# A mixing stage with its score and logarithm steps one cell ahead, and a convolution that starts in the pair before it

## The reference, cut to what matters

```python
h = rms_norm(x, norm_mix_g); proj = h @ w_in          # -> conv_in (2048), q, k, v (1024 each), gate logits (2048)
# branch 1: convolution
u = a * sigmoid(gt)                                    # a, gt: the halves of conv_in
y[c, t] = bias[c] + sum_{i<31} w[i, c] * u[c, t-30+i]  # 31 taps, each channel by itself
# branch 2: stick-breaking attention, 16 heads of 64, per query block
z = (q @ k.T) / 8                                      # causal: key < query
log_1m = where(causal, -softplus(z), 0)
after = reverse_cumsum(log_1m) - log_1m                # over the later keys
w = where(causal, exp(log_sigmoid(z) + after), 0)
o = w @ v
```

## Time and profile before

| | us |
|---|---|
| median of 3 runs | 4964.03 (4961.4 to 4964.75) |
| profiled execution, its own time | 4961.57 |
| its span, first to last instruction | 4959.8 |
| mean granted TensorE clock (of full speed) | 0.964 |
| the last output of the mixing stage is copied at | 1158.35 |

### The profile page before, as it was taken

The page is one execution under the profiler, slowest core; times in us unless marked ns, Lnnn a source line. Parts: engine busy times, 40 slices in busy tenths (PEclk is TensorE's granted clock), DMA queues, the critical chain, the costliest instruction groups (busy, mean ns, idle before and its releaser), DMA issues. The chain is left out here.

```text
span 4959.8 us, 62173 instructions
## 1 busy us (share of the span) xinstructions
PE 4612.5 (93%) x21768; PEld 3671.5 (74%) x21768; DVE 2884.2 (58%) x4467; ACT 1703.9 (34%) x2690; POOL 1781.3 (36%) x1078
## 2 busy tenths in 40 slices
PE   6999999986896987999999998999799999999998
PEld 5666666653676765888888887888688888888886
DVE  3777777776425217777777746776344444444445
ACT  3555555553524313333333333444112111111212
POOL 1443433341124115777777761111122222222221
PEclk9999999987998998999999999999899999999999
DMA  2111111103423131222222224555744444444441
GB/s 78 35 47 48 47 44 43 47 18 128 153 97 132 34 127 69 99 97 93 98 97 93 104 106 144 205 204 210 275 149 134 148 145 144 144 148 145 138 144 68
DMA packets 260002, 555.58 MB, mean 112 GB/s; under 512 B 17104, under 2 KB 148432, under 8 KB 246736
## 3 DMA queue, kind: packets, MB, share of 16 engines
q1 hardware_dynamic: 255184, 485.85, 29.1%
q10 hardware_dynamic: 4608, 67.11, 3.3%
HBM read 384.08 MB, written 168.82 MB: 111 GB/s over the span
## 5 line engine op out<-in xcount | busy, mean ns | idle before, releaser
L155 PE MATMUL expert_o<-expert_ahi,expert_vhi 128*128 128x512 f32 x2048 | 799.5, 390 | 25.8 <-POOL expert_vlo L2338 20.8
L156 PE MATMUL expert_o<-expert_alo,expert_vhi 128*128 128x512 f32 x2048 | 798.5, 390 | 0.0
L157 PE MATMUL expert_o<-expert_ahi,expert_vlo 128*128 128x512 f32 x2048 | 798.3, 390 | 0.0
L2402 DVE TENSOR_TENSOR expert_acc<-expert_acc,expert_o 128x512 f32<-128x512 f32 x496 | 341.0, 688 | 709.8 <-PE expert_o L157 704.7
L2338 POOL TENSOR_TENSOR expert_vlo<-expert_vraw,expert_vhi 128x1024 fp32r<-128x1024 f32 x128 | 323.3, 2526 | 1055.8 <-ACT expert_vhi L2356 1055.8
L155 PEld LDWEIGHTS expert_o<-expert_ahi,expert_vhi 128*128 128x128 f32 x2048 | 385.4, 188 | 108.1 <-issue 27.2
L156 PEld LDWEIGHTS expert_o<-expert_alo,expert_vhi 128*128 128x128 f32 x2048 | 385.5, 188 | 80.2 <-issue 0.2
L157 PEld LDWEIGHTS expert_o<-expert_ahi,expert_vlo 128*128 128x128 f32 x2048 | 385.5, 188 | 80.2
L155 PE MATMUL mix_gemm<-mix_hhi,mix_w_hi 128*128 128x512 f32 x896 | 373.8, 417 | 20.5 <-POOL mix_w_lo L185 13.5
L2362 ACT ACTIVATE expert_ahi<-expert_act 128x1024 fp32r<-128x1024 f32 x128 | 135.8, 1061 | 730.2 <-DVE expert_act L2392 730.2
L556 DVE SCALAR_TENSOR_TENSOR mix_room<-mix_u,mix_cwj,mix_room 128x1024 f32<-128x1024 f32 x240 | 361.3, 1505 | 6.1 <-DVE mix_u L528 3.2
(11 more groups left out here) (319 smaller groups left out, 9983.4 us busy)
## 6 DMA issues: line engine op xcount, KB each, us to landing
gates<-spread_stage ACTq DMA_DIRECT2D x32, 2048.0 KB, 15.0
expert_act<-gelu_u SPq DMA_DIRECT2D x128, 512.0 KB, 3.4
expert_graw<-gates SPq DMA_DIRECT2D x128, 512.0 KB, 4.6
expert_vraw<-in_peer_v SPq DMA_DIRECT2D x128, 512.0 KB, 6.5
select_raw<-in_select_pairs SPq DMA_DIRECT2D x54, 1024.0 KB, 5.0
gelu_u<-front SPq DMA_DIRECT2D x184, 256.0 KB, 2.0
mix_w_raw<-in_w_mix SPq DMA_DIRECT2D x56, 512.0 KB, 3.7
spread_uraw<-in_peer_u SPq DMA_DIRECT2D x36, 512.0 KB, 4.8
```

The lines of the kernel that those rows point to most:

```text
L155: nc.tensor.matmul(out, whi, xhi, start=(first and i == 0), stop=False)
L156: nc.tensor.matmul(out, whi, xlo, start=False, stop=False)
L157: mm = nc.tensor.matmul(out, wlo, xhi, start=False, stop=(last and i == len(terms) - 1))
L2402: nc.vector.tensor_tensor(acc[:, k, h * H:h * H + H], acc[:, k, h * H:h * H + H], ops[:, d, h], ALU.add).then_inc(added, 1)
```

## The change

It has four parts, all within `mixer_phase`.

1. ACT: Abs, Exp and Ln of cell n+1 (`log_part`) are issued in cell n, behind the high part of sp and the copies of finished projection groups, and ahead of wt = exp(lw) of cell n. The first cell's are issued before the cells begin. At the end of a pair this is cell 0 of the pair after it.
2. PE: in each cell the scores of the next cell (`z_cell`) are issued ahead of `add_own` of this cell, not behind it.
3. DVE: both log sigmoids (ls) are issued directly behind the softplus, and the low part of head 1 behind both; before, it stood between the two.
4. DVE: the 31 taps of every pair are shifted 16 places earlier. The first 16 taps of pair 0 (EARLY) run before the cells begin, and the cells of a pair hold its taps 16 to 30 and then taps 0 to 15 of the pair after it. The last pair holds only its own last 15 taps: one in cell 0, two in each of cells 1 to 7, none in cells 8 to 11. The tap weights `cwj` get a second buffer.

No arithmetic is added, and no DMA. The number of taps, matmuls and activations stays as it was.

```diff
-        cwj = m.sb("cwj", [P, TAPS + 1])
+        cwj = m.sb("cwj", [P, 2, TAPS + 1])
...
         TAPS_AT = [(0, 2)] + [(1, 2)] * 9 + [(1, 1), (0, 0)]
+        LAST_TAPS_AT = [(0, 1)] + [(1, 1)] * 7 + [(0, 0)] * 4
+        EARLY = TAPS - sum(map(sum, LAST_TAPS_AT))
...
+            def log_part(n, a):
+                for s in range(2):
+                    act.wait_ge(z_done[s], n + 1)
+                    nc.scalar.activation(expz[:, s, a:H], zps[:, s, a:H], ACT.Abs).then_inc(act_step[s], 1)
+                for s in range(2):
+                    act.wait_ge(act_step[s], n * 2 + 1)
+                    act.wait_ge(ls_done[s], n + 1)
+                    nc.scalar.activation(expz[:, s, a:H], expz[:, s, a:H], ACT.Exp, scale=-1.0).then_inc(act_step[s], 1)
+                for s in range(2):
+                    act.wait_ge(act_step[s], n * 2 + 2)
+                    nc.scalar.activation(ln[:, s, a:H], expz[:, s, a:H], ACT.Ln, bias=1.0).then_inc(ln_done[s], 1)
+
+            log_part(0, col0[0])
+
             def body(j, par, jj, more):
                 for i in range(NCELL):
                     a, n = col0[i], NCELL * j + i
-                    (the same Abs, Exp and Ln of cell n stood here)
                     for s in range(2):
                         act.wait_ge(sp_done[s], n + 1)
                         act.wait_ge(sp_used[s], n + 1)
                         ... sp_hi
                     if more and i:
                         for g in ends[i - 1]:
                             evict(*following(j, par, jj), g, more)
+                    if more or i < NCELL - 1:
+                        log_part(n + 1, col0[(i + 1) % NCELL])
                     ... wt = exp(lw)
...
+            def convs(j, par, jj, more, start, count):
+                for t in range(start + EARLY, start + EARLY + count):
+                    if t < TAPS:
+                        conv(j, par, jj, t)
+                    else:
+                        conv(*following(j, par, jj), t - TAPS)
...
+            for t in range(EARLY):
+                conv(0, 0, 0, t)
...
                     for s in range(2):
+                        dve.wait_ge(lw_done[s], n + 1)
                         nc.vector.scalar_tensor_tensor(out=ls[:, s, a:H], ...).then_inc(ls_done[s], 1)
-                        if s == 0:
-                            low_part(dve, nc.vector, j, 1, i)
-                    before = sum(map(sum, TAPS_AT[:i]))
-                    for t in range(before, before + TAPS_AT[i][0]):
-                        conv(j, par, jj, t)
+                    low_part(dve, nc.vector, j, 1, i)
+                    taps_at = TAPS_AT if more else LAST_TAPS_AT
+                    before = sum(map(sum, taps_at[:i]))
+                    convs(j, par, jj, more, before, taps_at[i][0])
...
-                    for t in range(before + TAPS_AT[i][0], before + sum(TAPS_AT[i])):
-                        conv(j, par, jj, t)
+                    convs(j, par, jj, more, before + taps_at[i][0], taps_at[i][1])
...
                 for i in range(NCELL):
                     for s in range(2):
-                        add_own(j, s, i)
-                    for s in range(2):
                         if i < NCELL - 1:
                             z_cell(j, par, s, i + 1)
                         elif more:
                             z_cell(j + 1, 1 - par, s, 0)
+                    for s in range(2):
+                        add_own(j, s, i)
```

More of the change, by code:

```diff
@@ L547, in conv @@
                 if t == 0:
-                    nc.vector.tensor_copy(cwj[:], cw[:, ds(j, 1), :].rearrange("p a t -> p (a t)")).then_inc(cwj_made, 1)
+                    nc.vector.tensor_copy(cwj[:, par], cw[:, ds(j, 1), :].rearrange("p a t -> p (a t)")).then_inc(cwj_made, 1)
                     dve.wait_ge(cwj_made, j + 1)
@@ L551, in conv @@
                     dve.wait_ge(u_made, 2 * j + 2 + 1)
-                    nc.vector.tensor_scalar(ybuf[:, par], u[:, par, 0:T], cwj[:, 0:1], cwj[:, TAPS:TAPS + 1],
+                    nc.vector.tensor_scalar(ybuf[:, par], u[:, par, 0:T], cwj[:, par, 0:1], cwj[:, par, TAPS:TAPS + 1],
                                             ALU.mult, ALU.add).then_inc(conv_step, 1)
@@ L555, in conv @@
                     dve.wait_ge(conv_step, TAPS * j + t)
-                    nc.vector.scalar_tensor_tensor(out=ybuf[:, par], in0=u[:, par, t:t + T], scalar=cwj[:, t:t + 1],
+                    nc.vector.scalar_tensor_tensor(out=ybuf[:, par], in0=u[:, par, t:t + T], scalar=cwj[:, par, t:t + 1],
                                                    in1=ybuf[:, par], op0=ALU.mult, op1=ALU.add).then_inc(conv_step, 1)
+            def convs(j, par, jj, more, start, count):
[4 more added lines that the diff above has]
+                        conv(*following(j, par, jj), t - TAPS)
             for h in range(2):
```

## The result

| | before | after |
|---|---|---|
| median of the runs, us | 4962.72 (4958.29 to 4964.75, 4 runs) | 4886.56 (4880.7 to 4886.78, 4 runs) |
| ratio, 95% interval | | 0.9845 (0.9828 to 0.9862) |
| profiled execution, own time / span | 4961.57 / 4959.8 | 4880.7 / 4879.0 |
| mean granted TensorE clock | 0.964 | 0.972 |
| last store of outputs in the mixing stage, start | 1158.97 | 1084.08 |

The kernel is 1.5% faster, 76.2 us by the medians. The prediction had 42.5 us less, and its range ended at 4893. (Before has one run more here than in the table ahead of the prediction.) In the profiled executions the mixing stage is 74.9 us shorter. The profiled span is 80.8 us shorter, but the 6 us behind the stage are not the change's: from the last store to the span's end the fourteen profiles of this study took between 3794.9 us (after) and 3802.4 us (e2), before 3800.8.

A forecast was written before the change was run, and what follows sets the result against it. PE was taken to bound projection pairs, the DVE and ACT chain the last pair. Savings of 21 + 13.5 + 3 + 5 = 42.5 us from 4961.57 give 4919.1, plus 2.5 for the median: 4921.5 us, range 4893 to 4950.

The forecast's parts named there:

- last pair: Last pair: sixteen fewer taps, with the logarithms, scores and log sigmoids moved, save 21 us; bounds 9.5 and 27.
- six ends of pairs, with the clock behind them: Pair ends before the last pair: earlier sp_hi and scores in PE's idle time save 13.5 us, the higher clock 3.
- cell 9, with the rest of the pair behind it: Cell 9 of projection pairs: the tap starting ahead of POOL's weight split saves 5 us; bounds 0 and 21.6.
- other cells: Other cells of the projection pairs: logarithms move into ACT's wait for lw, so nothing gained or lost.
- start of pair 0: Before the first softplus: sixteen taps run in DVE's idle 37.62 us and cost nothing.
- I take a quarter: Cell 9: of at most 21.6 us over six pairs, a quarter was counted, 5 us.
- The 0.9 us by which `add_own` comes later: Cell 9: `add_own`, now behind the scores, comes 0.9 us later, counted against the tap's 0.1 to 0.2 us lead.
- TensorE's clock: Projections behind pair ends: fewer at the lower clock, saving 3 us; bounds 0 and 12.
- the 1 us to be given back behind cell 10: Last pair: sp_hi of cell 11 queues behind wt of cell 10, losing about 1 us.
- Rival B: Last pair: the mask chain binds, so cells 0 to 7 gain nothing; 4932 us, chance 0.17.
- A: Pair ends and cell 9: the clock stays up and the tap wins its race; 68 us less, 4896 us, chance 0.19.
- D: Projection pairs: wt comes late and PE waits up to 1 us in each of 84 cells; 5006 us, chance 0.04.

The follow-up runs named there:

- e2: The kernel after without the sixteen early taps; logarithms, scores and log sigmoids stay ahead: 4900.33 us, 0.9876 of before.
- e6: The kernel after with DVE's low part of sp back between the two log sigmoids: 4950.64 us, 0.9981 of before.
- e5: The kernel after with `add_own` ahead of the next cell's scores again in every cell: 4952.63 us, 0.9988 of before.
- e3: The kernel before with only the next cell's scores moved ahead of `add_own` on PE: 5011.0 us, 1.0097 of before.
- e10: The kernel after with `add_own` ahead of the scores again in each pair's first cell only: 4893.43 us, 0.9871 of before.
- e7: The kernel after with sp_hi of the next pair's first cell ahead of the last output copies on ACT: 4874.77 us, 0.9831 of before.

## Why the prediction was wrong

The direction was right; the gain was forecast at 42.5 us and is 74.9 us in the profiled stage, 32.4 more. Term by term, from the cut of all pairs:

| term | forecast | measured |
|---|---|---|
| last pair | 21 | 24.6 |
| six ends of pairs, with the clock behind them | 16.5 | 24.8 |
| cell 9, with the rest of the pair behind it | 5 | 18.1 |
| other cells | 0 | 6.9 |
| start of pair 0 | 0 | 0.5 |

**The step that failed is cell 9: "I take a quarter, since the tap must win by tenths of a microsecond".** It is 13.1 of the 32.4 us. The mechanism and the price were near: 3.6 us a pair from pairs 3 and 6, and measured 4.1 in cell 9, of which 1.3 came back in the rest. What was mis-sized is the share of pairs in which the tap wins. The race was not a toss: it was won in every pair that splits weights there. I had the tap 0.1 to 0.2 us sooner; it gained 0.61 us on POOL (in pair 3 from 0.09 behind to 0.52 ahead, and about as much in the others). Behind the softplus DVE had waited for sp_hi with a log sigmoid of 0.68 us still to do; now that runs in the wait. e6 shows that in the kernel after this order alone decides the race; it was not run alone on the kernel before. The 0.9 us by which `add_own` comes later, which I set against it, doesn't touch the tap. Over seven pairs cell 9 gave 24.7 us, and the rest of the pair took 6.6 back. A likely cause is the same collision further on: the first tap behind lw now begins 1.87 us into the split and takes 2.22 us in pair 3, and DVE comes later to cell 10. No run shows how much that is.

By the Trainium skill (SBUF — State Buffer, section SBUF: two separate sides) the shared port pair of DVE and GpSimd is an exclusive lock, held for a whole instruction by whoever starts first. The rows agree: started first, the split takes 2.37 us and the tap 3.37; started second, the split takes 3.01 and the tap 1.27. The ties of pairs 0, 2 and 4 before don't show who had the lock first by their recorded starts; there the tap took 3.45. By that rule a race pays all or nothing; a quarter of six could only come from pairs that race differently, and here all six went the same way.

**TensorE's clock was sized at 3 us of at most 12.** With the term for the ends it is 8.3 us too small. At the start of pair 3, 5.4 us shorter, three pieces add up: sp_hi earlier 1.9 us, as forecast; the scores out of the way, with `add_own` at the higher clock, 1.5 us where I had 0.62 (from `add_own` to the first projection 0.51 us, and 1.98 before, 533.71 to 535.69); and twelve projections in 3.03 and not 5.09 us, 2.1 us. Plain starts won in the mean 5.3 us, pair 6's 4.1, and the two turns 2.4. Over all six ends the time from the store to `add_own` fell by 10.8 us (11.5 forecast), from there to the first projection by 7.6 (3.7), and the twelve projections by 6.4: 7.5 at the four ends without a turn, where the clock now stays up, and 1.1 lost at the turns. The 2.1 us set against these, for wt behind the logarithms, lie in the rest of the pairs: PE waited 3.1 us there for wt, in 6 times. That the turns keep their low clock was forecast rightly.

**The other cells.** I costed PE's order at nothing. It gives 0.12 us a cell (87.70 to 86.71 us over eight), and e5 takes it back. The scores have another shape than `add_own` and the projections, 64 rows and not 128; that the shape is the reason is not shown apart from the order. In a cell with 384 columns PE gets from the first of `add_own` or scores to the first projection in 1.72 us after,

```profile
576.29 0.51 PE L155 MATMUL mix_z<-mix_q_hi,mix_k_hi 64*128 64x512 f32 x2
...
577.21 0.44 PE L664 MATMUL mix_c<-mix_sp_hi,mix_tri 128*128 128x384 f32 x1
...
578.01 0.39 PE L155 MATMUL mix_gemm<-mix_hhi,mix_w_hi 128*128 128x512 f32 x1
```

and in 1.81 us before, with the scores between the two.

**The last pair** was right in its steps. Cells 0 to 7 lost 11.0 us (10.7 forecast), cells 8 to 10 take 6.25 us (6.6), with 1.02 us of waiting for scores (1 assumed); the 1 us to be given back behind cell 10 didn't come (from cell 11's softplus to the store 8.4 us, before 8.6). The pair's first softplus begins 2.5 us ahead of the store of outputs at its start (1004.33 and 1006.86), where it began 1.1 us behind it: 3.6 us earlier, not 1.9. Rival B fell: the 18 masks on wt between 960 and 1070 us take 0.64 us in the mean, not 1.32, and ACT waits for masks on sp as before, 7.9 us in all against 6.9. PE's waits for masks on wt rose from 3.6 to 7.8 us.

**The start** was right: the sixteen taps ran from 96.19 to 122.87 us, and the first softplus came at 133.70 us, where it had been at 133.66. Three of the taps began during a split and took 3.30 us, twelve others 1.28.

**The rivals.** What happened is A, given 0.19: 68 us by its own sum. The stage came out higher by the cells' order (6.9 us) and the last pair (3.6), and lower in cell 9 with the rest (18.1 and not 21.6) and, since turns keep the low clock, a little at the ends (24.8 and not 25.5). D didn't happen, but its warning was placed wrongly: PE waits not for wt but, in e3, for log sigmoids. I had not worked out what the scores themselves wait for.

The largest thing missed is that the parts don't add. Against before, the parts done alone give -3 (taps, not told from nothing), +7 (logarithms) and +51 us (scores); the scores with the log sigmoids -20, with the logarithms too -60, with the taps too -76. The log sigmoids alone were not run. Taking the scores or the log sigmoids out of the whole loses 70 and 64 of the stage's 74.9 us. A sum of separate gains describes this change only as a cut by place, not by edit.

What stays open is what decides the clock: with one idle piece of 1.55 to 1.59 us it fell at some ends and not at another (e10), and with one of 2.50 to 2.52 us it fell at one turn and not at the other (e7).

## What to carry to other kernels

When an instruction moves ahead in a queue, list what it waits for itself, its output buffer's last readers too, and move those as well: the scores ahead cost 50 us until the log sigmoids that read their PSUM stood together. Two instructions that lock each other out are a race with two outcomes; work out which one starts first and price that, not a mean. Cut all the pairs of a stage at the same few instructions before summing: it shows at once which places changed in every pair and which kernels differ where.

## What was not expected of the hardware

- A turn of the loop costs some 2.5 us of idle time on PE and DVE (2.54 and 2.38 us where pair 4 begins, after). How long the idle piece is doesn't tell whether the clock falls behind it: behind 2.52 us it stayed up, behind 2.50 us it fell (e7).
- `add_own` and the projections with the scores, of another shape, between them cost 0.1 us more than with the scores ahead of both: 1.81 against 1.72 us for the same ten matmuls.
- Of sixteen taps beside three splits, three took 3.30 us and the rest 1.28 (the first, of another form, 0.81), and the splits went from 2.39 to 2.88 us: a collision falls on single instructions and doesn't slow all of them a little.
- Two instructions whose recorded starts are within 0.03 us of each other went the same way each time: the tap lost to the split (3.45 to 3.48 us, before).
